# Splitting 512-column matmuls into two of 256 that accumulate in one half of a PSUM bank

## The chip, the cores and the metric

The kernel runs on one core of one Trainium2 chip. The metric is device time of one execution, in microseconds. The core's engines work side by side and wait for each other by semaphores: TensorE (PE in the profile; its weight loads are listed apart as PEld), VectorE (DVE), ScalarE (ACT), GpSimd (POOL) and SyncE (SP), whose queue issues most of the loads from memory.

## The reference

Two layers of a bidirectional encoder on 256 tokens of width 2048, all in float32:

```python
for l in range(DEPTH):
    h = rmsnorm(x, norm_mix[l])
    q, k, v, gate_b, gate_c, u = jnp.split(h @ w_in[l], splits, axis=-1)   # 1024 columns each
    q, k = apply_rope(q), apply_rope(k)                                    # 16 half heads of 64
    o_attn = diff_attention(q, k, v, lam)     # 8 heads: softmax 1 - lam * softmax 2, times v
    o_attn = rmsnorm(o_attn, subln[l]) * (1.0 - lam_init)
    z = gate_c * u
    o_conv = gate_b * (w[0] * z[t - 1] + w[1] * z[t] + w[2] * z[t + 1])    # centred, 3 taps
    x = x + concatenate([o_attn, o_conv]) @ w_out[l]
    h = rmsnorm(x, norm_ffn[l])
    x = x + (silu(h @ w_gate[l]) * (h @ w_up[l])) @ w_down[l]
return rmsnorm(x, norm_final)
```

## The kernel before

**Exactness.** Matmuls run on operands of type fp32r, which keeps fewer bits than float32. Each operand is therefore kept as two parts, a high one (the value rounded to fp32r) and a low one (value minus high part). A product is hi x hi + hi x lo + lo x hi. For weights, ScalarE makes the high part (`whi`) and VectorE the low one (`wlo`). The normed activations stand in `xg`, which holds for each of the 16 slices of the model's width 512 columns: 256 tokens of the high part, then 256 tokens of the low part.

**Blocks and banks.** Work is cut in blocks of 512 output columns. Each layer has 4 blocks for q and k, 2 for v, 6 for the conv path (named gate: two for B, two for C, two for u), 4 for the output projection, and then those of the feed-forward part. A block reads its weights in units of two 128-row slices. PSUM has 8 banks of 512 columns; blocks use banks 0 to 3, the attention and transposes banks 4 to 7.

**Two kinds of product.** The v, output and feed-forward blocks go by tokens (`products_by_tokens`, L2118): activations are the loaded operand, weights stream through in 512 columns, and the result has tokens on partitions. The q/k and gate blocks go by features (`products`, L2092): a 128 x 128 tile of weights is loaded and the tokens stream through, so the result has features on partitions, 4 tiles in 4 banks. There the high weights meet all 512 columns of `xg` at once (L2108): hi x hi lands in the left half of the bank, hi x lo in the right half. The low weights meet only the 256 high columns (L2111), which add to the left half. For every slice TensorE does the two tiles of a pair with high weights, then the same two with low weights; first tiles 0 and 1 for a unit, then 2 and 3.

**Leaving the bank.** The two halves must be added. `low_halves` (L978) on ScalarE copies the right half of each tile's bank to `ev`; `sums` (L1664) on VectorE adds left half and `ev`, into `qk` for a q/k block and into `ev` for a gate block. For B and C, `gate_out` (L1740) then multiplies by the token's RMS factor into `gates`; for u, `conv_products` (L1746) multiplies by the gated C to give z. Each of these steps is counted up on a semaphore: `low_copied`, `bank_free`, `gate_stored`, `z_ready`.

**Order.** The order on each engine is written out by hand; every engine runs its list in order. A block's drain stands in the lists of ScalarE and VectorE behind the splits of the first two units of the next block. TensorE waits in `tile_free` (L2088) before it starts a pair of tiles: the counter `bank_free`, counted up by every last reader of a bank, must have reached the number of tiles up to the one four tiles earlier. In a gate block the attention of one head (mix, scores, two kinds of transposes) is put between units, and VectorE makes sums of feed-forward weights ahead of time (`sums_ahead`, L1380) that ScalarE's queue stores to memory: in some gate blocks one such sum stands between the second and the third tile of the drain. The POOL's queue swaps rows of `qk` for the rotary embedding once a block's drain has been counted (`swap`, L772).

Of the kernel before, what the change touches and what calls it, by code (L numbers as in the profile page):

```python
# [9 lines left out]
ALU = mybir.AluOpType  # L10
# [4 lines left out]
S = 256  # L15
# [146 lines left out]
class Block:  # L162
# [5 lines left out]
    def __init__(self, plan, layer, name, i, by_tokens, units):  # L168
        self.layer, self.name, self.i = layer, name, i
        self.by_tokens, self.units = by_tokens, units  # L170
        self.tiles = QT if by_tokens else BT
        self.tile0, self.low0 = plan.tiles, plan.lows
        plan.tiles += self.tiles
        plan.lows += 0 if by_tokens else BT
        self.load, self.split = {}, {}
        self.first_unit = None
        self.ahead = {}
# [98 lines left out]
class Plan:  # L276
    def __init__(self):
        self.tiles = self.lows = self.units_taken = self.quads = self.pair_count = self.fold_steps = 0

        self.ready_at = []  # L280
        self.by_dve = self.by_pool = 0
# [49 lines left out]
    def split_unit(self, loads, tiles, block=None, last=False, by_pool=False):  # L331
# [22 lines left out]
        else:  # L354
            self.by_dve += 1
            self.ready_at.append(("dve", self.by_dve))
        return n

    def next_place(self):
# [15 lines left out]
def build_program(nc, x, x_t_d, w_in, w_out, w_gu, w_down, consts_d, lambdas_d, tables_d, ident_d, gain_d, out):  # L375
# [146 lines left out]
    first_half_hi = sem("first_half_hi")  # L522
    low_copied = sem("low_copied")
    xg_hi = sem("xg_hi")
# [24 lines left out]
    first_half_ready = sem("first_half_ready")  # L549
    bank_free = sem("bank_free")  # L550
    set_up = sem("set_up")
    warm_set = sem("warm_set")
# [7 lines left out]
    rope_done = sem("rope_done")  # L560
    gate_stored = sem("gate_stored")
    z_ready = sem("z_ready")
    conv_step = sem("conv_step")
# [42 lines left out]
    def wait_for_split(engine, n):  # L606
        kind, count = plan.ready_at[n]
        engine.wait_ge(pool_weights_ready if kind == "pool" else weights_ready, count)

    def batch_number(layer, name, b=0):  # L610
# [17 lines left out]
    with nc.Block() as block:  # L628
# [138 lines left out]
        def _(pool):  # L767
# [4 lines left out]
            def swap(layer, c):  # L772
                blk = at_block[layer, "qk", c]
                pool.wait_ge(bank_free, blk.tile0 + BT)
                if layer * NQK + c > 1:
                    pool.wait_ge(rope_done, layer * NQK + c - 1)
                for r in range(4):
                    pool.dma_start(swaps[c % 2][32 * r:32 * r + 32],
                                   qk[32 * (r ^ 1):32 * (r ^ 1) + 32, c * BT:(c + 1) * BT, :]
                                   ).then_inc(swap_landed[c % 2], 16)  # L780
# [109 lines left out]
        def _(act):  # L890
# [86 lines left out]

            def low_halves(blk, ev_free=None):  # L978
                if ev_free is not None:
                    act.wait_ge(ev_free[0], ev_free[1])  # L980
                for j in range(BT):
                    act.wait_ge(tile_done, blk.tile0 + j + 1)
                    act.activation(ev[:, j, :], bank[blk.bank(j)][:, S:2 * S], ACT.Copy).then_inc(low_copied, 1)

            def squares(norm, c):
                for q in range(QT):
                    if norm == 0:
                        act.wait_ge(x_landed[q], 16)
                    else:
                        act.wait_ge(bank_free, chunk_source(norm, c).tile0 + q + 1)  # L990
                    before = norm * QT * NCH + QT * c + q
# [26 lines left out]
            def conv(layer, u):  # L1018
                for j in range(BT):
                    tap = layer * (3 * CT) + (C_CONV + CT + BT * u + j)  # L1020
                    act.wait_ge(z_ready, layer * CT + (BT * u + j + 1))
                    act.activation(ev[:, j, :], gates[:, CT + BT * u + j, :], ACT.Copy, scale=consts[:, tap:tap + 1]
# [7 lines left out]
            def silu(layer, g, q):  # L1030
# [6 lines left out]
                elif g > 1:  # L1037
                    act.wait_ge(hidden_turned, layer * NGU + g - 1)
                act.wait_ge(bank_free, blk.tile0 + q + 1)
                act.activation(ev[:, QT * (g % 2) + q, :], gate_up_tile(layer, g, q)[:, 0:S], ACT.Silu, scale=rms_tok[:, q:q + 1]  # L1040
# [132 lines left out]

            def gates_stored(layer, n):
                return gate_stored, layer * (2 * CT) + n

            act.dma_start(consts[:], consts_d).then_inc(consts_landed, 16)
# [4 lines left out]
            for layer in range(DEPTH):  # L1182
# [28 lines left out]
                for c in range(1, NQK):  # L1211
                    blk = at_block[layer, "qk", c]
                    split(blk, 0, 2)
                    low_halves(at_block[layer, "qk", c - 1])
                    if layer == 0 and c == 1:
# [11 lines left out]
                split(blk, 0, 2)  # L1227
                low_halves(at_block[layer, "qk", NQK - 1])
                split(blk, 2, UNITS)
# [9 lines left out]
                for b in range(3 * NG):  # L1239
# [5 lines left out]
                    copy_weights(layer, h - 1)  # L1245
                    if b == 1:
                        low_halves(at_block[layer, "gate", 0])
                    elif b > 1:
                        low_halves(at_block[layer, "gate", b - 1], gates_stored(layer, min(b - 1, 2 * NG) * BT))
                    split(blk, 2, 4)  # L1250
# [13 lines left out]
                copy_weights(layer, HEADS - 1)  # L1264
                low_halves(at_block[layer, "gate", 3 * NG - 1], (conv_ready, layer * CT + BT))
                split(blk, 2, 4)
                conv(layer, 1)
                split(blk, 4, 6)
# [95 lines left out]
        def _(dve):  # L1364
# [298 lines left out]

            def sums(blk, qk_block=None, between=None):  # L1664
                for j in range(BT):
                    if j == BT // 2 and between is not None:
                        sums_ahead(between, 1, range(3), 1)
                    dst = ev[:, j, :] if qk_block is None else qk[:, qk_block * BT + j, :]
                    dve.wait_ge(low_copied, blk.low0 + j + 1)
                    dve.tensor_tensor(dst, bank[blk.bank(j)][:, 0:S], ev[:, j, :], ALU.add).then_inc(bank_free, 1)  # L1670

            def rotate(layer, c):
# [66 lines left out]

            def gate_out(layer, g, scale):  # L1740
                blk = at_block[layer, "gate", g]
                for j in range(BT):
                    dve.wait_ge(bank_free, blk.tile0 + j + 1)
                    dve.tensor_tensor(gates[:, g * BT + j, :], ev[:, j, :], scale[:], ALU.mult).then_inc(gate_stored, 1)

            def conv_products(layer, u):  # L1746
                dve.wait_ge(gate_stored, (layer + 1) * 2 * CT)
                for j in range(BT):
                    t = CT + BT * u + j
                    dve.wait_ge(bank_free, at_block[layer, "gate", 2 * NG + u].tile0 + j + 1)  # L1750
                    dve.tensor_tensor(gates[:, t, :], ev[:, j, :], gates[:, t, :], ALU.mult).then_inc(z_ready, 1)

# [107 lines left out]
            for layer in range(DEPTH):  # L1860
# [25 lines left out]
                for c in range(1, NQK):  # L1886
                    blk = at_block[layer, "qk", c]
                    split(blk, 0, 2)
                    if layer == 0 and c == 2:
                        norm_sums(mix)  # L1890
                    sums(at_block[layer, "qk", c - 1], c - 1)
                    sums_ahead(blk, 1, range(3))
# [17 lines left out]
                sums_ahead(blk, 1, range(3))  # L1910
                sums(at_block[layer, "qk", NQK - 1], NQK - 1)
                split(blk, 2, 3)
# [27 lines left out]
                for b in range(1, 2 * NG + 1):  # L1940
                    blk = at_block[layer, "gate", b]
                    split(blk, 0, 2)
                    sums_ahead(blk, 1, range(3))
                    sums(at_block[layer, "gate", b - 1], between=blk)
                    split(blk, 2, 3)
                    gate_out(layer, b - 1, rms_bc if b <= NG else rms2_bc)
                    split(blk, 3, 4)
                    attention_part(layer, blk, b + 2)
                blk = at_block[layer, "gate", 3 * NG - 1]
                split(blk, 0, 2)  # L1950
                sums_ahead(blk, 1, range(3))
                sums(at_block[layer, "gate", 2 * NG])
                split(blk, 2, 3)
                conv_products(layer, 0)
                split(blk, 3, 4)
                conv_neighbours(layer, 0)
# [11 lines left out]
                sums_ahead(blk, 1, range(3))  # L1968
                sums(at_block[layer, "gate", 3 * NG - 1])
                split(blk, 2, 3)  # L1970
                conv_products(layer, 1)
                split(blk, 3, 4)
                conv_neighbours(layer, 1)
# [110 lines left out]
        def _(pe):  # L2084
# [3 lines left out]
            def tile_free(blk, j):  # L2088
                if blk.tile0 + j >= BT:
                    pe.wait_ge(bank_free, blk.tile0 + j + 1 - BT)  # L2090

            def products(blk, ks, moving, halves=range(UNIT_KT)):  # L2092
# [4 lines left out]
                for pair in range(0, BT, 2):  # L2097
# [5 lines left out]
                    for k in ks:  # L2103
                        for i in halves:
                            kt = UNIT_KT * k + i
                            final = k == blk.units - 1 and i == UNIT_KT - 1
                            for j in js:
                                pe.matmul(b[j][:], whi[:, plan.span[blk.split[k]].start + i, w[j]], moving[:, kt, :], start=(kt == 0),  # L2108
                                          stop=False, skip_group_check=True)
                            for j in js:  # L2110
# [138 lines left out]
            def turn_x(norm, c):  # L2249
                pe.wait_ge(bank_free, chunk_source(norm, c).tile0 + QT)  # L2250
                for i in range(BT):
# [38 lines left out]
            def mix(layer, h):  # L2290
                n = layer * HEADS + h
                pe.wait_ge(wt_copied, n + 1)
                if h == 0:

                    pe.wait_ge(bank_free, at_block[layer, "v", 0].tile0 + QT)
                else:
# [287 lines left out]
```

## Time and profile before

| | us |
|---|---|
| median of 3 runs | 2151.37 (2151.27 to 2151.44) |
| the profiled execution | 2151.05 |
| its span, first to last instruction | 2149.3 |

A row of a timeline names the start, the length, the engine, the line and the shapes (output <- inputs, the loaded operand last); xN merges N like instructions that follow each other. The length of a matmul includes the time until its result is out, so matmuls overlap and the distance of two starts tells the pace. In groups by line, busy is the time covered by the group's instructions and the mean is that of one.

### The profile page before, as it was taken

To read this page: it belongs to the slowest core of one execution; us is meant where nothing else is said; L and a number is where in the kernel's file an instruction comes from. 1 tells how busy PE (TensorE), PEld (TensorE's weight loads), DVE (VectorE), ACT (ScalarE), POOL (GpSimd) and SP (SyncE) were. 2 spreads that over 40 slices of the span, in tenths; PEclk is the share of its full clock that TensorE was granted. 3 is DMA by queue.
4 is the path that set the end of the run, shared out by engine and by line. 5 is a ranking of instruction groups with operands and counts; after the bars stand their busy time and mean duration, and the time that the engine had idled before them with its cause. 6 is when DMAs were issued, how large, how long until landed. Compare 5 with 4: busy or idle time off the path is not lost.

```text
span 2149.3 us, 27652 instructions
## 1 busy us (share of the span) xinstructions
PE 2138.9 (100%) x10349; PEld 1783.9 (83%) x10349; DVE 1851.8 (86%) x2149; ACT 1244.7 (58%) x1652; POOL 313.8 (15%) x298
## 2 busy tenths in 40 slices
PE   9999999999999999999999999999999999999998
PEld 7888888788888888888888888888888888888886
DVE  6788887899999988999867788878999998988997
ACT  6445455566666655556554555546666666655564
POOL 0031120211121110000001211202112112000010
PEclk9999999999999999999999999999999999999999
DMA  9768877877786876767757688678678777757685
GB/s 351 241 255 338 335 254 281 270 261 243 268 284 219 279 261 204 228 216 225 239 198 252 253 326 333 247 286 294 222 275 278 248 259 265 254 192 223 218 240 181
DMA packets 171877, 553.25 MB, mean 257 GB/s; under 512 B 19552, under 2 KB 20192, under 8 KB 166752
## 3 DMA queue, kind: packets, MB, share of 16 engines
q1 hardware_dynamic: 149040, 479.33, 62.1%
q0 software_dynamic: 16512, 31.47, 8.3%
q10 hardware_dynamic: 6192, 40.69, 4.7%
q8 instruction: 82, 1.34, 0.2%
q14 instruction: 51, 0.42, 0.0%
HBM read 507.37 MB, written 39.85 MB: 255 GB/s over the span
## 4 chain that ended last, share of the span: by engine, by line
PE 98%; DVE 1%; ACT 0%; issue 0%; ACTq 0%; DVEq 0%
PE bank L2135 15%; PE bank L2136 15%; PE bank L2137 15%; PE bank L2108 14%; PE bank L2148 10%; PE bank L2149 10%; PE bank L2150 10%; PE bank L2111 7%; PE bank L2318 1%; PE bank L2277 1%; PE bank L2300 1%; DVE wlo L1398 1%; PE bank L2256 0%; PE bank L2286 0%; PE bank L2247 0%; PE bank L2307 0%
## 5 line engine op out<-in xcount | busy, mean ns | idle before, releaser
L902 ACT ACTIVATE whi<-raw 128x1024 fp32r<-128x1024 f32 x472 | 484.6, 1056 | 196.2 <-PE bank L2137 109.6
L1390 DVE TENSOR_TENSOR wlo<-raw,whi 128x1024 fp32r<-128x1024 f32 x446 | 538.2, 1231 | 69.0 <-ACT whi L902 68.0
L917 ACT ACTIVATE whi<-raw 128x1024 fp32r<-128x1024 f32 (+1 forms) x368 | 390.4, 1088 | 211.9 <-DVE raw L1413 90.3
L1398 DVE TENSOR_TENSOR wlo<-raw,whi 128x1024 fp32r<-128x1024 f32 (+1 forms) x368 | 452.3, 1260 | 34.6 <-ACT whi L917 31.4
L2108 PE MATMUL bank<-xg,whi 128*128 128x512 f32 x1280 | 407.0, 399 | 0.0
L2135 PE MATMUL bank<-whi,xg 128*128 128x512 f32 x736 | 289.8, 394 | 0.0
L2111 PEld LDWEIGHTS bank<-xg,wlo 128*128 128x128 f32 x1280 | 240.5, 188 | 56.9
L2137 PE MATMUL bank<-whi,xg 128*128 128x512 f32 x736 | 287.0, 390 | 0.0
L2136 PE MATMUL bank<-wlo,xg 128*128 128x512 f32 x736 | 286.8, 390 | 0.0
L2111 PE MATMUL bank<-xg,wlo 128*128 128x256 f32 x1280 | 252.2, 278 | 0.0
L2108 PEld LDWEIGHTS bank<-xg,whi 128*128 128x128 f32 x1280 | 195.1, 189 | 2.4 <-DVE xg L1695 0.7
L2135 PEld LDWEIGHTS bank<-whi,xg 128*128 128x128 f32 x736 | 138.2, 188 | 29.5 <-DVE wlo L1390 1.4
L2135 PE MATMUL bank<-whi,hidden 128*128 128x512 f32 x416 | 162.6, 391 | 0.0
L2137 PEld LDWEIGHTS bank<-whi,xg 128*128 128x128 f32 x736 | 138.2, 188 | 29.0
L2137 PE MATMUL bank<-whi,hidden 128*128 128x512 f32 x416 | 162.0, 389 | 0.0
L2136 PE MATMUL bank<-wlo,hidden 128*128 128x512 f32 x416 | 161.9, 389 | 0.0
L2136 PEld LDWEIGHTS bank<-wlo,xg 128*128 128x128 f32 x736 | 138.3, 188 | 27.6
L2148 PE MATMUL bank<-whi,form_hi_gu 128*128 128x512 f32 x400 | 155.7, 389 | 0.0
L2150 PE MATMUL bank<-whi,form_lo_gu 128*128 128x512 f32 x400 | 155.7, 389 | 0.0
L2149 PE MATMUL bank<-wlo,form_hi_gu 128*128 128x512 f32 x400 | 155.7, 389 | 0.0
L809 POOL DMA_DIRECT2D raw<-w_gu_dram x52 | 45.9, 884 | 561.9 <-DMA raw<-w_gu_dram 507.9
L2148 PE MATMUL bank<-whi,xg 128*128 128x512 f32 x300 | 119.9, 400 | 0.8 <-DVE wlo L1398 0.7
(172 smaller groups left out, 3554.9 us busy)
## 6 DMA issues: line engine op xcount, KB each, us to landing
raw<-w_gu_dram SPq DMA_DIRECT2D x252, 512.0 KB, 6.3
raw<-w_in_dram SPq DMA_DIRECT2D x188, 512.0 KB, 4.7
raw<-w_down_dram SPq DMA_DIRECT2D x140, 512.0 KB, 5.3
sums_kept<-raw ACTq DMA_DIRECT2D x32, 1024.0 KB, 4.0
raw<-w_out_dram SPq DMA_DIRECT2D x64, 512.0 KB, 4.5
raw_gu<-w_gu_dram SPq DMA_DIRECT2D x64, 512.0 KB, 6.4
raw<-w_gu_dram SPq DMA_DIRECT2D x124, 256.0 KB, 5.6
raw<-sums_kept SPq DMA_DIRECT2D x44, 512.0 KB, 5.1
```

The source lines that it names most:

```text
L902: act.activation(whi[:, plan.span[blk.split[k]]], raw_place(slot)[:, half * UNIT_KT:(half + 1) * UNIT_KT, :], ACT.Copy).then_inc(hi_ready, 1)
L917: act.activation(whi[:, plan.span[quad.split[n]]], raw_place(place)[:, tiles, :], ACT.Copy).then_inc(hi_ready, 1)
L1390: dve.tensor_tensor(wlo[:, tiles], raw_place(slot)[:, half * UNIT_KT:(half + 1) * UNIT_KT, :], lo_bits(whi[:, tiles]), ALU.subtract).then_ ...
L1398: dve.tensor_tensor(wlo[:, into], raw_place(place)[:, tiles, :], lo_bits(whi[:, into]), ALU.subtract).then_inc(weights_ready, 1)
L2108: pe.matmul(b[j][:], whi[:, plan.span[blk.split[k]].start + i, w[j]], moving[:, kt, :], start=(kt == 0), stop=False, skip_group_check=True)
L2111: done = pe.matmul(b[j][:, 0:S], wlo[:, plan.span[blk.split[k]].start + i, w[j]], moving[:, kt, 0:S], start=False, stop=final, skip_group_ ...
L2135: pe.matmul(b[:], x_hi, w_hi, start=(n == UNIT_KT * blk.first_unit), stop=False)
L2136: pe.matmul(b[:], x_hi, w_lo, start=False, stop=False)
L2137: done = pe.matmul(b[:], x_lo, w_hi, start=False, stop=final)
L2148: pe.matmul(into[:], x_hi, w_hi, start=start, stop=False)
L2149: pe.matmul(into[:], x_hi, w_lo, start=False, stop=False)
L2150: return pe.matmul(into[:], x_lo, w_hi, start=False, stop=stop)
```

## The change

`products` issues, for each slice and tile, two matmuls of 256 columns with the same high weights, one with the high and one with the low half of `xg`, and both add to the left half of the bank. Each has its own weight load. The right half is not used any more. So `low_halves` and `sums` go: for q and k, ScalarE copies the left half straight to `qk` (`copy_out`); for B and C, VectorE's `gate_out` reads the bank; for u, `conv_products` reads the bank. The split of the third unit moves from ahead of these products to behind them. `low_copied`, `gate_stored` and `z_ready` go; a bank is now freed on one of two counters, `bank_copied` (ScalarE, q/k blocks) or `bank_free` (VectorE, all others), and `wait_for_bank` picks the one and its count for a tile.

```diff
@@ class Block / class Plan
-        self.tile0, self.low0 = plan.tiles, plan.lows
+        self.tile0 = plan.tiles
         plan.tiles += self.tiles
-        plan.lows += 0 if by_tokens else BT
+        for _ in range(self.tiles):
+            plan.free_at.append(plan.next_free("scalar" if name == "qk" else "vector"))
...
+    def next_free(self, engine):
+        self.freed[engine] += 1
+        return engine, self.freed[engine]
...
+    def wait_for_bank(engine, tile):
+
+        by, count = plan.free_at[tile]
+        engine.wait_ge(bank_copied if by == "scalar" else bank_free, count)
...
@@ POOL
             def swap(layer, c):
                 blk = at_block[layer, "qk", c]
-                pool.wait_ge(bank_free, blk.tile0 + BT)
+                wait_for_bank(pool, blk.tile0 + BT - 1)
...
@@ ScalarE
-            def low_halves(blk, ev_free=None):
-                if ev_free is not None:
-                    act.wait_ge(ev_free[0], ev_free[1])
+            def copy_out(blk):
                 for j in range(BT):
                     act.wait_ge(tile_done, blk.tile0 + j + 1)
-                    act.activation(ev[:, j, :], bank[blk.bank(j)][:, S:2 * S], ACT.Copy).then_inc(low_copied, 1)
+                    act.activation(qk[:, blk.i * BT + j, :], bank[blk.bank(j)][:, 0:S], ACT.Copy).then_inc(bank_copied, 1)
...
             def conv(layer, u):
...
-                    act.wait_ge(z_ready, layer * CT + (BT * u + j + 1))
+                    wait_for_bank(act, at_block[layer, "gate", 2 * NG + u].tile0 + j)
...
-                    low_halves(at_block[layer, "qk", c - 1])
+                    copy_out(at_block[layer, "qk", c - 1])
...
-                    if b == 1:
-                        low_halves(at_block[layer, "gate", 0])
-                    elif b > 1:
-                        low_halves(at_block[layer, "gate", b - 1], gates_stored(layer, min(b - 1, 2 * NG) * BT))
...
                 copy_weights(layer, HEADS - 1)
-                low_halves(at_block[layer, "gate", 3 * NG - 1], (conv_ready, layer * CT + BT))
                 split(blk, 2, 4)
+                act.wait_ge(conv_ready, layer * CT + BT)
                 conv(layer, 1)
...
@@ VectorE
-            def sums(blk, qk_block=None, between=None):
...
-            def gate_out(layer, g, scale):
+            def gate_out(layer, g, scale, between):
+
                 blk = at_block[layer, "gate", g]
                 for j in range(BT):
-                    dve.wait_ge(bank_free, blk.tile0 + j + 1)
-                    dve.tensor_tensor(gates[:, g * BT + j, :], ev[:, j, :], scale[:], ALU.mult).then_inc(gate_stored, 1)
+                    if j == BT // 2:
+                        sums_ahead(between, 1, range(3), 1)
+                    dve.wait_ge(tile_done, blk.tile0 + j + 1)
+                    dve.tensor_tensor(gates[:, g * BT + j, :], bank[blk.bank(j)][:, 0:S], scale[:], ALU.mult
+                                      ).then_inc(bank_free, 1)
 
             def conv_products(layer, u):
...
-                    dve.wait_ge(bank_free, at_block[layer, "gate", 2 * NG + u].tile0 + j + 1)
-                    dve.tensor_tensor(gates[:, t, :], ev[:, j, :], gates[:, t, :], ALU.mult).then_inc(z_ready, 1)
+                    dve.wait_ge(tile_done, blk.tile0 + j + 1)
+                    dve.tensor_tensor(gates[:, t, :], bank[blk.bank(j)][:, 0:S], gates[:, t, :], ALU.mult
+                                      ).then_inc(bank_free, 1)
...
-                    sums(at_block[layer, "qk", c - 1], c - 1)
...
                     split(blk, 0, 2)
                     sums_ahead(blk, 1, range(3))
-                    sums(at_block[layer, "gate", b - 1], between=blk)
-                    split(blk, 2, 3)
-                    gate_out(layer, b - 1, rms_bc if b <= NG else rms2_bc)
-                    split(blk, 3, 4)
+                    gate_out(layer, b - 1, rms_bc if b <= NG else rms2_bc, blk)
+                    split(blk, 2, 4)
...
@@ TensorE
             def tile_free(blk, j):
                 if blk.tile0 + j >= BT:
-                    pe.wait_ge(bank_free, blk.tile0 + j + 1 - BT)
+                    wait_for_bank(pe, blk.tile0 + j - BT)
...
                             for j in js:
-                                pe.matmul(b[j][:], whi[:, plan.span[blk.split[k]].start + i, w[j]], moving[:, kt, :], start=(kt == 0),
-                                          stop=False, skip_group_check=True)
+                                for part in (0, S):
+                                    pe.matmul(b[j][:, 0:S], whi[:, plan.span[blk.split[k]].start + i, w[j]],
+                                              moving[:, kt, part:part + S], start=(kt == 0 and part == 0), stop=False,
+                                              skip_group_check=True)
                             for j in js:
                                 done = pe.matmul(b[j][:, 0:S], wlo[:, plan.span[blk.split[k]].start + i, w[j]], moving[:, kt, 0:S],
                                                  start=False, stop=final, skip_group_check=True)
```

## Rows read from the trace of the kernel before

**Rows 1.** The page, part 1: busy us (share) and instructions, by engine.

```profile
PE 2138.9 (100%) x10349; PEld 1783.9 (83%) x10349; DVE 1851.8 (86%) x2149; ACT 1244.7 (58%) x1652; POOL 313.8 (15%) x298
```

**Rows 2.** The page, part 4: the chain that ended last, by engine.

```profile
PE 98%; DVE 1%; ACT 0%; issue 0%; ACTq 0%; DVEq 0%
```

**Rows 3.** The chain of waits by line, whole span.

```profile
by line: PE bank L2135 14.8%; PE bank L2136 14.7%; PE bank L2137 14.7%; PE bank L2108 14.0%; PE bank L2148 10.1%; PE bank L2149 9.9%; PE bank L2150 9.9%; PE bank L2111 6.9%; PE bank L2318 0.9%; PE bank L2277 0.7%; PE bank L2300 0.7%; DVE wl
```

**Rows 4.** Instructions by line: shapes, count | busy us, mean ns | idle.

```profile
L2108 PE MATMUL bank<-xg,whi 128*128 128x512 f32 x1280 | 407.0, 399 | 0.0
L2111 PE MATMUL bank<-xg,wlo 128*128 128x256 f32 x1280 | 252.2, 278 | 0.0
L2111 PEld LDWEIGHTS bank<-xg,wlo 128*128 128x128 f32 x1280 | 240.5, 188 | 56.9
L2300 PEld LDWEIGHTS bank<-v_tok,wt 128*128 128x128 f32 x128 | 15.8, 191 | 0.3
```

**Rows 5.** Stages: length, busy PE, PEld, DVE, ACT, POOL, clock, DMA.

```profile
1098.93:1121.22 22.29, 22.29 (x131) 19.45 (x129) 14.39 (x15) 9.47 (x12) 2.03 (x4) 1.00 0.67 228
169.32:194.32 25.00, 25.00 (x156) 21.88 (x155) 21.37 (x34) 13.04 (x27) 4.50 (x6) 1.00 0.89 336
```

**Rows 6.** Timeline of TensorE (start us, length us), one step of that q/k block.

```profile
1098.93 0.63 PE L2108 MATMUL bank<-xg,whi 128*128 128x512 f32 x2
1099.39 0.40 PE L2111 MATMUL bank<-xg,wlo 128*128 128x256 f32 x2
1099.62 0.40 PE L2108 MATMUL bank<-xg,whi 128*128 128x512 f32 x1
```

**Rows 7.** Timeline of TensorE's weight loads, the mix of a head and what follows.

```profile
174.78 0.97 PEld L2300 LDWEIGHTS bank<-v_tok,wt 128*128 128x128 f32 x8
175.67 0.30 PEld L2108 LDWEIGHTS bank<-xg,whi 128*128 128x128 f32 x2
```

**Rows 8.** Timeline of TensorE, products by tokens, a start and the twelfth after it.

```profile
101.26 0.39 PE L2135 MATMUL bank<-whi,xg 128*128 128x512 f32 x1
...
103.98 0.39 PE L2135 MATMUL bank<-whi,xg 128*128 128x512 f32 x1
```

**Rows 9.** Timeline of TensorE, scores of a head, second pair and last pair.

```profile
153.91 0.28 PE L2277 MATMUL bank<-k_lo,q_hi 64*128 64x256 f32 x2
...
154.38 0.28 PE L2277 MATMUL bank<-k_hi,q_lo 64*128 64x256 f32 x2
```

**Rows 10.** Instructions grouped by line, the drains of the banks.

```profile
L983 ACT ACTIVATE ev<-bank 128x256 f32<-128x256 f32 x80 | 26.4, 382 | 97.1 <-PE bank L2111 97.1
L1670 DVE TENSOR_TENSOR ev<-bank,ev 128x256 f32<-128x256 f32 x48 | 18.0, 418 | 11.5 <-ACT ev L983 11.3
L1670 DVE TENSOR_TENSOR qk<-bank,ev 128x256 f32<-128x256 f32 x32 | 12.1, 419 | 30.1 <-ACT ev L983 30.1
L1744 DVE TENSOR_TENSOR gates<-ev,rms_bc 128x256 f32<-128x256 f32 x32 | 11.4, 417 | 0.0
L1751 DVE TENSOR_TENSOR gates<-ev,gates 128x256 f32<-128x256 f32 x16 | 5.7, 418 | 0.0
```

**Rows 11.** Timelines of VectorE and TensorE where one gate block follows another.

```profile
1261.41 0.76 DVE L1670 TENSOR_TENSOR ev<-bank,ev 128x256 f32<-128x256 f32 x2 [0.77 <-ACT ev L983]
1264.66 0.75 DVE L1670 TENSOR_TENSOR ev<-bank,ev 128x256 f32<-128x256 f32 x2
1263.63 0.62 PE L2108 MATMUL bank<-xg,whi 128*128 128x512 f32 x2
1266.42 0.40 PE L2108 MATMUL bank<-xg,whi 128*128 128x512 f32 x1
```

**Rows 12.** Timelines of VectorE and TensorE at the output projection's start, layer 0.

```profile
293.92 1.26 DVE L1670 TENSOR_TENSOR ev<-bank,ev 128x256 f32<-128x256 f32 x3
294.03 0.39 PE L2111 MATMUL bank<-xg,wlo 128*128 128x256 f32 x2
294.48 0.47 PE L2135 MATMUL bank<-whi,mixed 128*128 128x512 f32 x1
```

More of the change, by code:

```diff
@@ L277, in __init__ @@
     def __init__(self):
-        self.tiles = self.lows = self.units_taken = self.quads = self.pair_count = self.fold_steps = 0
+        self.tiles = self.units_taken = self.quads = self.pair_count = self.fold_steps = 0
+        self.free_at, self.freed = [], {"scalar": 0, "vector": 0}
         self.ready_at = []
@@ L522, in build_program @@
     first_half_hi = sem("first_half_hi")
-    low_copied = sem("low_copied")
     xg_hi = sem("xg_hi")
@@ L550, in build_program @@
     bank_free = sem("bank_free")
+    bank_copied = sem("bank_copied")
     set_up = sem("set_up")
@@ L560, in build_program @@
     rope_done = sem("rope_done")
-    gate_stored = sem("gate_stored")
-    z_ready = sem("z_ready")
     conv_step = sem("conv_step")
@@ L989, in squares @@
                     else:
-                        act.wait_ge(bank_free, chunk_source(norm, c).tile0 + q + 1)
+                        wait_for_bank(act, chunk_source(norm, c).tile0 + q)
                     before = norm * QT * NCH + QT * c + q
@@ L1038, in silu @@
                     act.wait_ge(hidden_turned, layer * NGU + g - 1)
-                act.wait_ge(bank_free, blk.tile0 + q + 1)
+                wait_for_bank(act, blk.tile0 + q)
                 act.activation(ev[:, QT * (g % 2) + q, :], gate_up_tile(layer, g, q)[:, 0:S], ACT.Silu, scale=rms_tok[:, q:q + 1]
@@ L1172, in head_out @@
                                ).then_inc(o_hi, 1)
-            def gates_stored(layer, n):
-                return gate_stored, layer * (2 * CT) + n
             act.dma_start(consts[:], consts_d).then_inc(consts_landed, 16)
@@ L1227, in _ @@
                 split(blk, 0, 2)
-                low_halves(at_block[layer, "qk", NQK - 1])
+                copy_out(at_block[layer, "qk", NQK - 1])
                 split(blk, 2, UNITS)
@@ L1662, in fold @@
                 dve.tensor_tensor(resid[:, :, right], resid[:, :, right], two, ALU.add).then_inc(fold_step, 1)
-            def sums(blk, qk_block=None, between=None):
[L1665 to L1670, printed above, removed]
             def rotate(layer, c):
@@ L1738, in v_out @@
                                       ALU.mult).then_inc(bank_free, 1)
-            def gate_out(layer, g, scale):
+            def gate_out(layer, g, scale, between):
                 blk = at_block[layer, "gate", g]
                 for j in range(BT):
-                    dve.wait_ge(bank_free, blk.tile0 + j + 1)
-                    dve.tensor_tensor(gates[:, g * BT + j, :], ev[:, j, :], scale[:], ALU.mult).then_inc(gate_stored, 1)
+                    if j == BT // 2:
[3 more added lines that the diff above has]
+                                      ).then_inc(bank_free, 1)
             def conv_products(layer, u):
-                dve.wait_ge(gate_stored, (layer + 1) * 2 * CT)
+                blk = at_block[layer, "gate", 2 * NG + u]
+                wait_for_bank(dve, at_block[layer, "gate", 2 * NG - 1].tile0 + BT - 1)
                 for j in range(BT):
                     t = CT + BT * u + j
-                    dve.wait_ge(bank_free, at_block[layer, "gate", 2 * NG + u].tile0 + j + 1)
-                    dve.tensor_tensor(gates[:, t, :], ev[:, j, :], gates[:, t, :], ALU.mult).then_inc(z_ready, 1)
+                    dve.wait_ge(tile_done, blk.tile0 + j + 1)
+                    dve.tensor_tensor(gates[:, t, :], bank[blk.bank(j)][:, 0:S], gates[:, t, :], ALU.mult
+                                      ).then_inc(bank_free, 1)
             def conv_neighbours(layer, u):
@@ L1910, in _ @@
                 sums_ahead(blk, 1, range(3))
-                sums(at_block[layer, "qk", NQK - 1], NQK - 1)
                 split(blk, 2, 3)
@@ L1951, in _ @@
                 sums_ahead(blk, 1, range(3))
-                sums(at_block[layer, "gate", 2 * NG])
-                split(blk, 2, 3)
                 conv_products(layer, 0)
-                split(blk, 3, 4)
+                split(blk, 2, 4)
                 conv_neighbours(layer, 0)
@@ L1968, in _ @@
                 sums_ahead(blk, 1, range(3))
-                sums(at_block[layer, "gate", 3 * NG - 1])
-                split(blk, 2, 3)
                 conv_products(layer, 1)
-                split(blk, 3, 4)
+                split(blk, 2, 4)
                 conv_neighbours(layer, 1)
@@ L2249, in turn_x @@
             def turn_x(norm, c):
-                pe.wait_ge(bank_free, chunk_source(norm, c).tile0 + QT)
+                wait_for_bank(pe, chunk_source(norm, c).tile0 + QT - 1)
                 for i in range(BT):
@@ L2293, in mix @@
                 if h == 0:
-                    pe.wait_ge(bank_free, at_block[layer, "v", 0].tile0 + QT)
+                    wait_for_bank(pe, at_block[layer, "v", 0].tile0 + QT - 1)
                 else:
```

## The prediction

> **What bounds the kernel now.** I read the page first: TensorE is busy for the whole span, VectorE for 86%, ScalarE for 58% [rows 1]. A share of busy time doesn't say who waits for whom, so the chain of waits comes next: 98% of the time that leads to the last instruction is TensorE's own [rows 2], and by line the two matmul lines which the change edits, L2108 and L2111, hold 14.0% and 6.9%, some 449 us [rows 3]. In the table by stage, the second q/k block of layer 1 takes 22.29 us with TensorE busy throughout, VectorE for 14.39 and ScalarE for 9.47 us, at the full clock level of 2.4 GHz (1.00 in the PEclk column). VectorE has 35% and ScalarE 58% of that block free, and in the second gate block of layer 0, where VectorE is busiest (21.37 of 25.00 us), TensorE is busy throughout as well [rows 5]. So what they lose is worth nothing while TensorE never waits for them, and the whole question is the time of TensorE's own instruction stream.
>
> **What one step of that stream takes.** A step is two output tiles at one 128-row slice of the contraction: two 512-column matmuls (L2108), then two 256-column ones (L2111). A block holds 16 slices x 2 tile pairs = 32 steps, so a step takes 22.29 / 32 = 696.6 ns; the kernel has 1280 / 2 = 640 steps [rows 4] (10 blocks in each of 2 layers), 446 us. Inside a step, from the starts in the timeline, the two long matmuls take 0.46 us and the two short ones 0.23 us [rows 6].
>
> **The change, part by part.**
>
> *The matmuls.* A step goes from 4 matmuls (512, 512, 256, 256 columns) to 6 of 256. The columns stay 1536, which is 640 ns at 2.4 GHz, and each matmul has its own weight load: loads and matmuls are equal in number now, 10349 of each [rows 1], though the products by tokens use the same weights twice in a row. So 1280 matmuls and 1280 loads are added. Are the loads hidden? The recorded load lasts 188 ns [rows 4], more than there is from one short matmul to the next. But in the mix, where a load is recorded at 191 ns [rows 4], 8 of them in a row start 0.89 us / 8 = 111 ns apart [rows 7], so a load doesn't hold the engine for its recorded time; 111 ns is under the 115 ns between short matmuls [rows 6]. They stay hidden, by only a few nanoseconds. If that cover went, 4 new or shortened matmuls a step would each wait for up to 188 - 111 = 77 ns more, 4 x 77 x 640 = 197 us; the short ones of today, which need a load each as well, show nothing like it.
>
> What does a 256-column matmul take in a long row of its kind? No row shows exactly that, so I bound it by four readings. (a) Half of a 512-column matmul in the products by tokens, whose starts are 2.72 / 12 = 226.7 ns apart: 113.3 [rows 8]. (b) The short ones as they stand, which come in twos behind two long ones: 0.23 / 2 = 115 by the starts, 6.9% of 2149.3 us / 1280 = 115.9 by the chain; I take 115.4 [rows 3, 6]. (c) The scores, the only run of 256-column fp32r matmuls one after another: two row groups at once, five starts 0.47 / 4 = 117.5 apart [rows 9]. (d) A fixed cost for every matmul: (696.6 - 640) / 4 = 14.2 ns, so 106.7 + 14.2 = 120.8. By (d) the 226.7 of the 512-column ones (213.3 + 13.4) fits almost exactly. Break-even is 696.6 / 6 = 116.1.
>
> I take (c), 117.5: it is the one row in which the pace must sustain itself. In (b) two short ones may run ahead and be paid back by the next long one; what makes me suspect it is that the long ones take 0.46 / 2 = 230 or more [rows 6], against 226.7 in the products by tokens [rows 8]. A step becomes 6 x 117.5 = 705.0 ns, +8.4, times 640: **+5.4 us**. The ends are 113.3 (-16.8 ns a step, -10.7 us) and 120.8 (+28.2, +18.1 us).
>
> *Draining the bank.* ScalarE loses 48 copies of a gate tile's low half at 0.382 us; the 32 copies for q and k stay, now as the whole drain and straight into qk. VectorE loses 80 additions at 0.418 (48 + 32); its 48 gate and conv products stay at 0.418 and read the bank in place of ev [rows 10]. Reading a bank costs no more: the additions that go read one, in the same 0.418. All of it lies beside TensorE, so I cost it at nothing. The cover is the time between a drain's end and the matmul that reuses the bank. At a gate boundary the additions for the first two tiles end at 1261.41 + 0.76 = 1262.17 and TensorE returns at 1263.63; those for the other two end at 1265.41 and TensorE starts them at 1266.42 [rows 11]. That is 1.46 and 1.01 us to spare. After the change each drain drops one hop (q and k end at ScalarE's copy; the gate product starts without waiting for one), so the spare time grows. In the gate blocks one prepared sum (three VectorE instructions) still stands between the second and third tile, as before; that it becomes the bound would take a delay of a full microsecond.
>
> *Two waits that can shrink.* At the start of the output projection TensorE waits for the first drain of the last gate block: the last pair of short matmuls starts at 294.03, the next line at 294.48, not 294.26, and the addition that frees the bank started at 293.92 [rows 12]. That is 0.22 us in each layer, 0.44 us at most to be had and, if conv_products gets there later by one such instruction, 0.84 to be lost. VectorE has four additions fewer to do in the block before; I take -0.2 us.
>
> *Waits.* No new one is added to TensorE: the wait on a freed bank moves to a counter of the engine that frees it. ScalarE's wait for conv_ready moves from ahead of low copies that are gone to the second conv, behind two splits; VectorE counts it up at the end of the block before; queued behind it on ScalarE are the convolution's middle taps and the splits from the fifth unit on. The POOL's row swaps for rope start on ScalarE's copy, about one addition (0.42 us) earlier. SP's loads and their order are untouched. What is late next is TensorE itself.
>
> **Sum.** +5.4 - 0.2 = +5.2 us. The profiled execution took 2151.05 us (span 2149.3, 1.75 around it) and becomes 2156.3; the median of the runs is 2151.37, 0.32 above, so I predict **2156.6 us**.
>
> **Rivals.**
>
> *Each matmul has a fixed cost (d).* 6 x 120.8 = 724.8, +18.1 us: 2169.3 with the waits. For it: one constant explains both the 226.7 [rows 8] and the 696.6 [rows 5] within 1 ns a matmul. Against it: short ones start 115 apart today, and the scores 117.5.
> The Trainium skill, TensorE: Matmul & The Clock Gate, section Back-to-back issue gap, gives the gap as the columns at 2.4 GHz plus about 2.5 ns for each matmul, whatever its length, which also speaks against splitting; by it the 1280 extra matmuls would add 3.2 us, an estimate, and the time would be 2154.4. The products by tokens show 13.4 ns over the columns, not 2.5 [rows 8], so its size doesn't hold here, while its form is the rival's.
>
> *Not slower: the pairs of today already show the sustained pace (b).* A load can start only when the matmul before it has started, so no debt is carried from one to the next and 115.4 holds through the block: 6 x 115.4 = 692.4, -4.2 ns a step, -2.7 us, and 2148.5. It decides as soon as the pace stays under 116.1. For it: it is the pace of these very blocks. Against it: the long ones' excess of some 4 to 6 ns each over those in the products by tokens [rows 6, 8].
>
> *Columns alone count (a).* The long ones' excess vanishes too: 680 a step, -10.7 us, 2140.5. Against it: nothing in these blocks runs at that pace today.
>
> *The lighter VectorE shows.* It can give only time in which TensorE waits. The chain has 2% outside TensorE [rows 2], and both blocks looked at have none [rows 5]; what I found is the 0.44 us [rows 12]. Not a case of its own.
>
> **Chances and range.** Pace near 117.5: 0.40 (2153.5 to 2159.5, from 116.8 to 118.4). Fixed cost: 0.27. Pace of the pairs: 0.24. Columns alone: 0.06. The rest, either way: 0.03. About 0.2% (4.3 us) is what a measurement tells from no change, so slower begins at 2155.7: just over half of the likeliest case, all of the fixed cost and a little of the rest make 0.50. The lower part of the likeliest case and three quarters of the pairs make 0.35, the rest 0.15. The range from 2145 to 2171 takes in the fixed cost and the pairs and leaves out columns alone.
>
> **What would show it.** In the profile after: the same q/k block [rows 5] longer than 22.29 us (22.56 for 117.5, 23.2 for a fixed cost, 22.16 for the pairs), with TensorE still busy throughout. Six starts in a step at an even distance. L2108's successor with 2560 matmuls of 256 columns and as many loads. VectorE's busy time down by about 80 x 0.418 = 33 us and ScalarE's by 18 us, with no gain from either. I am wrong if TensorE shows waits on the freed bank inside the gate blocks, if the loads stand alone on the chain, or if a block takes less than 22.2 us.

## The result and the profile after

The changed kernel takes 2165.1 us (2165.02 to 2165.14, 3 runs) against 2151.37: ratio 1.0064, 95% interval 1.0041 to 1.0087. It is slower by 13.7 us, as forecast in sign and within the range, but by more than twice the 5.2 us that I gave; the time lies next to the rival of a fixed cost (2169.3).

The page of the changed kernel, parts 1 and 4, which answer to [rows 1, 2]:

```profile
PE 2152.1 (99%) x11629; PEld 1854.7 (86%) x11629; DVE 1822.6 (84%) x2069; ACT 1231.6 (57%) x1604; POOL 302.5 (14%) x298
...
PE 97%; DVE 2%; ACT 0%; issue 0%; DMA 0%; ACTq 0%; DVEq 0%
```

There are 1280 matmuls and 1280 loads more. VectorE is busy for 29 us less and ScalarE for 13 us less, and neither buys anything: 97% of the chain is TensorE's, 98% before. By line [rows 3]:

```profile
by line: PE bank L2127 14.5%; PE bank L2129 14.5%; PE bank L2128 14.4%; PE bank L2099 14.3%; PE bank L2140 9.8%; PE bank L2142 9.6%; PE bank L2141 9.6%; PE bank L2103 7.1%; DVE wlo L1398 1.0%; PE bank L2310 0.9%; PE bank L2269 0.7%; PE bank
```

L2099 is the successor of L2108, L2103 of L2111. Together they hold 21.4% of 2163.2 us, 463 us, where they held 449. In groups by line, with the drains (L990 copies q and k, L1739 makes the gates), for [rows 4, 10]:

```profile
L2099 PE MATMUL bank<-xg,whi 128*128 128x256 f32 x2560 | 416.1, 285 | 0.5 <-DVE wlo L1693 0.5
L2099 PEld LDWEIGHTS bank<-xg,whi 128*128 128x128 f32 x2560 | 352.5, 192 | 2.6 <-DVE xg L1687 0.9
L2103 PE MATMUL bank<-xg,wlo 128*128 128x256 f32 x1280 | 257.7, 283 | 0.0
L2103 PEld LDWEIGHTS bank<-xg,wlo 128*128 128x128 f32 x1280 | 199.5, 192 | 0.0
...
L1739 DVE TENSOR_TENSOR gates<-bank,rms_bc 128x256 f32<-128x256 f32 x32 | 12.0, 417 | 4.5 <-PE bank L2103 4.5
L990 ACT ACTIVATE qk<-bank 128x256 f32<-128x256 f32 x32 | 10.5, 381 | 48.8 <-PE bank L2103 48.8
```

The idle column shows the direction: the drains wait for TensorE, and TensorE's products wait 0.5 us in all, at the kernel's start. The two stages of [rows 5], with the same columns:

```profile
1106.52:1129.56 23.04, 23.04 (x194) 23.04 (x193) 12.94 (x11) 9.47 (x12) 2.03 (x4) 1.00 0.64 219
173.07:198.74 25.67, 25.67 (x221) 25.40 (x220) 20.11 (x30) 12.07 (x23) 4.51 (x6) 1.00 0.93 347
```

The q/k block takes 0.75 us longer, the gate block 0.67, both with TensorE busy throughout. If every block grew as the one of its kind that is shown, eight q/k blocks and twelve gate blocks make 8 x 0.75 + 12 x 0.67 = 14.0 us; 0.44 us of waits are gone, which leaves 13.6 of the 13.9 us by which the span grew. The timeline of TensorE, at the start of the output projection [rows 12] and in a q/k block [rows 6]:

```profile
301.16 0.40 PE L2103 MATMUL bank<-xg,wlo 128*128 128x256 f32 x2
301.40 0.40 PE L2127 MATMUL bank<-whi,mixed 128*128 128x512 f32 x1
...
1109.16 0.40 PE L2103 MATMUL bank<-xg,wlo 128*128 128x256 f32 x2
1109.40 0.64 PE L2099 MATMUL bank<-xg,whi 128*128 128x256 f32 x4
1109.88 0.40 PE L2103 MATMUL bank<-xg,wlo 128*128 128x256 f32 x2
```

Two starts are 0.24 us from the next kind, four 0.48: 120 ns each, and 32 x 6 x 120.0 = 23.04 us is the whole block. The old short matmuls were 115 apart. At 301 us the line after the last pair follows at once; the wait of 0.22 us is gone.

### The profile page after: what moved, and what is told of

It is laid out like the page before. It is cut to its first block, busy times and chain, and to the rows that moved or that the text cites. A ratio compares the mean times of both kernels' runs of the same rounds, so it can differ in the third digit from the quotient of the medians.

```text
span 2163.2 us, 30076 instructions
## 1 busy us (share of the span) xinstructions
PE 2152.1 (99%) x11629; PEld 1854.7 (86%) x11629; DVE 1822.6 (84%) x2069; ACT 1231.6 (57%) x1604; POOL 302.5 (14%) x298
## 4 chain that ended last, share of the span: by engine, by line
PE 97%; DVE 2%; ACT 0%; issue 0%; DMA 0%; ACTq 0%; DVEq 0%
PE bank L2127 15%; PE bank L2129 14%; PE bank L2128 14%; PE bank L2099 14%; PE bank L2140 10%; PE bank L2142 10%; PE bank L2141 10%; PE bank L2103 7%; DVE wlo L1398 1%; PE bank L2310 1%; PE bank L2269 1%; PE bank L2292 1%; PE bank L2248 0%; PE bank L2278 0%; ACT whi L926 0%
## 5 line engine op out<-in xcount | busy, mean ns | idle before, releaser
L2099 PE MATMUL bank<-xg,whi 128*128 128x256 f32 x2560 | 416.1, 285 | 0.5 <-DVE wlo L1693 0.5
L2099 PEld LDWEIGHTS bank<-xg,whi 128*128 128x128 f32 x2560 | 352.5, 192 | 2.6 <-DVE xg L1687 0.9
L2103 PE MATMUL bank<-xg,wlo 128*128 128x256 f32 x1280 | 257.7, 283 | 0.0
L2103 PEld LDWEIGHTS bank<-xg,wlo 128*128 128x128 f32 x1280 | 199.5, 192 | 0.0
```

What stands on the lines that cost most here:

```text
L2099: pe.matmul(b[j][:, 0:S], whi[:, plan.span[blk.split[k]].start + i, w[j]], moving[:, kt, part:part + S], start=(kt == 0 and part == 0), st ...
L2103: done = pe.matmul(b[j][:, 0:S], wlo[:, plan.span[blk.split[k]].start + i, w[j]], moving[:, kt, 0:S], start=False, stop=final, skip_group_ ...
```

## The experiments

Three theories, made after the result, stand against each other. Theory A, the rival of a fixed cost with its size taken from [rows 8]: an fp32r matmul costs its columns at 2.4 GHz and a fixed 13.3 ns. Theory B: columns cost 17/16 of their time, and a row of loads sustains one in 120 ns. Theory C: the drain has a part in it. Each kernel ran beside the kernel before on the same chip.

**The matmuls split alone.** On the kernel before; each half of the bank is opened with a start flag of its own, which changes the sums in q, k and the gates, not the stream of instructions:

```diff
-                                pe.matmul(b[j][:], whi[...], moving[:, kt, :], start=(kt == 0), ...)
+                                for part in (0, S):
+                                    pe.matmul(b[j][:, part:part + S], whi[...], moving[:, kt, part:part + S], start=(kt == 0), ...)
```

> The kernel before with only the matmuls split: each 512-column one becomes two of 256, which write the two halves of the bank as before, so the drain with its second addition stays. Theory A, a fixed cost for every matmul (a 256-column one takes 106.7 + 13.3 = 120.0 ns in a long row, a 512-column one 213.3 + 13.3 = 226.7): the whole rise comes from here, the q/k block of 22.29 us takes 23.04, and the time is 2165.5 us, the changed kernel's 2165.1 and the 0.4 us of two waits at the output projection that stay. Theory B, a row of loads with nothing long between them sustains one in 120 ns, while columns cost 17/16 of their time: the same 23.04 us and 2165.5. Theory C, part of the rise comes from the new drain (a bank freed later, a wait on two counters): below 2164, by that part.

Measured: 2165.51 us, ratio 1.0064 (1.0052 to 1.0077). The stage of a q/k block:

```profile
1107.15:1130.19 23.04, 23.04 (x195) 23.04 (x193) 14.46 (x15) 9.48 (x12) 2.03 (x4) 1.00 0.63 215
```

The whole rise is here, with the old drain and VectorE at 14.46 us, against 14.39 before [rows 5]. C falls.

**The drain alone.** On the changed kernel:

```diff
-                                for part in (0, S):
-                                    pe.matmul(b[j][:, 0:S], whi[...], moving[:, kt, part:part + S], ...)
+                                pe.matmul(b[j][:], whi[...], moving[:, kt, :], start=(kt == 0), ...)
```

> The changed kernel with the matmuls of the kernel before: 512 columns into the whole bank, while the drain reads the left half alone, so high weights times low activations is left out of q, k and the gates. Theories A and B: the drain is worth only the waits at the output projection, 2150.9 us, 0.4 under before, and q/k blocks stay at 22.29 us. Theory C: above 2152.5.

Measured: 2151.45 us, ratio 0.9999 (0.9990 to 1.0008): no change that the runs can tell. Two stages, and the start of the output projection in the timeline:

```profile
1098.56:1120.85 22.29, 22.29 (x130) 19.45 (x129) 12.88 (x11) 9.48 (x12) 2.03 (x4) 1.00 0.67 228
169.25:194.25 25.00, 25.00 (x157) 21.88 (x155) 20.09 (x30) 11.97 (x23) 4.51 (x6) 1.00 0.90 339
```

```profile
293.96 0.39 PE L2101 MATMUL bank<-xg,wlo 128*128 128x256 f32 x2
294.19 0.40 PE L2125 MATMUL bank<-whi,mixed 128*128 128x512 f32 x1
```

Both blocks keep their length to 0.01 us. 294.19 - 293.96 = 0.23, where it was 0.45 [rows 12]: the trace shows the 0.22 us that the total is too coarse to show.

**320 columns, and 384.** On the changed kernel, N = 320 or 384:

```diff
-                                for part in (0, S):
-                                    pe.matmul(b[j][:, 0:S], whi[...], moving[:, kt, part:part + S], ...)
+                                pe.matmul(b[j][:, 0:N], whi[...], moving[:, kt, 0:N], start=(kt == 0), ...)
...
-                                done = pe.matmul(b[j][:, 0:S], wlo[...], moving[:, kt, 0:S], ...)
+                                done = pe.matmul(b[j][:, 0:N], wlo[...], moving[:, kt, 0:N], ...)
```

> The changed kernel with four matmuls of 320 columns in a step (high weights and low weights each meet the first 320 columns of the activations) in place of six of 256: part of high times low is left out, and a part of low times low is added that the drain doesn't read. A length between 256 and 512 tells a fixed cost from a share of the columns. Theory A: 133.3 + 13.3 = 146.7 ns each, a step 586.7, a q/k block 18.77 us, in all 2151 - 640 x 110 ns = 2081 us. Theory B: 133.3 x 17/16 = 141.7 ns each (over the 120 of a load), a step 566.7, a block 18.13 us, 2068 us.

> As with 320 columns, with 384: four matmuls a step that see the first 384 columns of the activations; part of high times low is left out. Theory A: 160 + 13.3 = 173.3 ns each, a q/k block without waits 32 x 693.3 ns = 22.19 us. A share of the columns (17/16): 170.0 ns, 21.76 us. The columns are as many as before (1536), and so are the matmuls of a step, so by theory A such blocks can't be shorter than 22.19 us in any mix of lengths.

Measured with 320: 2102.22 us, ratio 0.977 (0.9752 to 0.9788), neither 2081 nor 2068. The stages say why; first a block without waits, then two others:

```profile
1072.92:1091.70 18.78, 18.78 (x131) 18.78 (x129) 12.76 (x11) 9.48 (x12) 2.03 (x4) 1.00 0.83 287
27.63:49.16 21.53, 19.33 (x131) 18.79 (x129) 9.77 (x10) 14.38 (x28) 2.22 (x4) 1.00 0.95 354
198.99:222.20 23.21, 22.55 (x161) 21.72 (x160) 20.70 (x31) 12.00 (x24) 4.51 (x6) 1.00 0.98 370
```

18.78 / 128 = 146.7 ns: A's figure to the last digit, not B's 141.7. In the others TensorE is no longer busy throughout, the DMA share is 0.95 and 0.98, and loads of weights (`raw<-w_in_dram`) stand on the chain of waits:

```profile
by line: PE bank L2125 15.2%; PE bank L2127 15.1%; PE bank L2126 15.0%; PE bank L2138 10.3%; PE bank L2140 10.1%; PE bank L2139 10.1%; PE bank L2098 3.1%; PE bank L2101 3.1%; DMA raw<-w_in_dram 3.0%; DVE wlo L1390 1.9%; DMA sums_kept<-raw 1
```

This much faster, TensorE outruns its weights, and most of the 21 us that are missing from A's sum are waits. The waits of TensorE (for which line, in all, times, longest) name the drain too:

```profile
PE bank L2098 <- DVE gates L1739: 7.0, 12, 1.0
PE bank L2098 <- DVE wlo L1390: 4.4, 5, 1.2
PE bank L2125 <- DVE gates L1748: 2.1, 2, 1.1
```

Of 18.1 us of such waits in all (1.9 in the kernel before), 9.5 are for VectorE's gate products and 7.4 for its splits of weights. In the gate block shown VectorE is busy for 20.70 of 23.21 us, so here, unlike in the kernel before, a lighter VectorE might be worth something. How much of the loss is the loads' and how much VectorE's, no run tells apart.

With 384, 2149.88 us in one run. The q/k block:

```profile
1098.25:1120.44 22.19, 22.19 (x130) 22.19 (x130) 12.85 (x11) 9.47 (x12) 2.03 (x4) 1.00 0.68 231
```

22.19 / 128 = 173.4 ns, where A has 173.3. With the 226.7 of 512 columns [rows 8] and the 120.0 of 256, four lengths lie on columns / 2.4 GHz + 13.3 ns, with a granted clock of 1.00 in the stages shown. B falls.

**Long and short in turn.** On the kernel before:

```diff
                             for j in js:
                                 pe.matmul(b[j][:], whi[...], moving[:, kt, :], ...)
-                            for j in js:
                                 done = pe.matmul(b[j][:, 0:S], wlo[...], moving[:, kt, 0:S], ...)
```

> The kernel before with the order inside a step changed from long, long, short, short to long, short, long, short; nothing is left out. Theory A: the four costs add up whatever their order, 693 to 697 ns a step, 2149.3 to 2151.6 us, although the starts may shift between long and short. Theory B: every load of a short one now lies behind a long one, so no load is late and only columns count: 2 x (226.7 + 113.3) = 680 ns a step, a q/k block of 21.8 us, 2140.7 us.

Measured: 2153.4 us, ratio 1.0008 (0.9999 to 1.0016). Two stages and a stretch of the timeline:

```profile
1100.91:1123.10 22.19, 22.19 (x131) 19.57 (x129) 14.49 (x15) 9.63 (x13) 2.03 (x4) 1.00 0.68 230
170.45:195.51 25.06, 25.06 (x156) 21.88 (x155) 21.40 (x34) 13.11 (x28) 4.52 (x6) 1.00 0.89 335
```

```profile
1109.92 0.39 PE L2108 MATMUL bank<-xg,whi 128*128 128x512 f32 x1
1110.15 0.28 PE L2110 MATMUL bank<-xg,wlo 128*128 128x256 f32 x1
1110.27 0.39 PE L2108 MATMUL bank<-xg,whi 128*128 128x512 f32 x1
```

The q/k block is 226.7 + 120.0 = 346.7 ns times 64, to the digit; B's 21.8 us is not there. The total lies above A's range, though. The gate block shown grew by 0.06 us, and the first two q/k blocks of layer 0 take 22.88 and 22.61 us, where the kernel before has 22.37 and 22.29. What the order changes there was not followed up.

**Long ones first, then four short ones.** On the kernel before:

```diff
                         for i in halves:
                             kt = UNIT_KT * k + i
-                            final = k == blk.units - 1 and i == UNIT_KT - 1
                             for j in js:
                                 pe.matmul(b[j][:], whi[...], moving[:, kt, :], ...)
+                        for i in halves:
+                            kt = UNIT_KT * k + i
+                            final = k == blk.units - 1 and i == UNIT_KT - 1
                             for j in js:
                                 done = pe.matmul(b[j][:, 0:S], wlo[...], moving[:, kt, 0:S], ...)
```

> The kernel before with the order changed inside a unit of two slices: its four long matmuls first, then its four short ones; nothing is left out. Theory A (every matmul costs its columns and 13.3 ns; a short one can start early behind a long one, and the next long one pays it back): the sum stays, 693 to 697 ns a step, a q/k block without waits 22.19 to 22.29 us, and in the row of four the later short ones come 120 ns apart, not 115. Theory D, which I took for the likeliest not-slower case (the pairs of the kernel before show the true cost of a short one): all four come 115 ns apart.

Measured: 2153.07 us, ratio 1.0007 (0.9997 to 1.0017). The timeline:

```profile
1110.39 1.09 PE L2107 MATMUL bank<-xg,whi 128*128 128x512 f32 x4
1111.32 0.64 PE L2113 MATMUL bank<-xg,wlo 128*128 128x256 f32 x4
1111.80 1.09 PE L2107 MATMUL bank<-xg,whi 128*128 128x512 f32 x4
```

Four short ones take 0.48 us, 120 each, not 115: the pairs of the kernel before did not show the true cost, and D, my not-slower rival, falls. But the four long ones take 0.93 us, 232.5 ns each, so A's sum fails here. The block:

```profile
1100.57:1123.03 22.46, 22.46 (x131) 19.63 (x129) 14.44 (x15) 9.47 (x12) 2.03 (x4) 1.00 0.66 226
```

That is 702 ns a step, where A allowed 693 to 697. A mix of lengths costs 0 to 9 ns a step over A's 693.3, by its order: 693.3 in turn, 696.6 as the kernel before has it, 702 grouped; equal lengths cost nothing over it. Why the order matters stays open.

**bf16.** On the changed kernel, all matmuls of a step read bf16, first as every second half-word with 256 and 320 columns, then side by side from one constant tile:

```diff
-                                    pe.matmul(b[j][:, 0:S], whi[..., w[j]], moving[:, kt, part:part + S], ...)
+                                    pe.matmul(b[j][:, 0:S], half(whi)[..., half_cols(P * j, P)], half(moving)[:, kt, half_cols(part, S)], ...)
```

> The changed kernel with the six matmuls of a step on bf16: each operand is read as the upper half-word of its four bytes (every second half-word), so the lower bits of all products by features are left out. If the 13.3 ns belong to fp32r: the pace falls to what the loads allow, 109 to 111 ns in the transposes and the mix of the kernel before, a step of at most 666 ns and a q/k block without waits of 21.3 us or less. If any matmul pays them: 120 ns and 23.04 us as in the changed kernel. If reading every second half-word is slow, above 120 ns, and nothing follows.

> Four matmuls of 320 columns in a step, as in the fp32r kernel of that length, on the upper half-words read as bf16; the lower bits and part of high times low are left out. With 256 columns bf16 took 113.3 ns, 6.7 over its columns. A fixed cost of the type: 133.3 + 6.7 = 140.0 ns, a q/k block without waits 32 x 560 = 17.92 us. A share of the columns (17/16): 141.7 ns, 18.13 us. A floor set by the loads at 113: 133.3 to 136 ns.

> The changed kernel with the six matmuls of a step on bf16 operands that lie side by side (one constant tile for weights and activations, from the first gate block on), so the products by features are left out there; the first q and k of layer 0 stay fp32r. If the 6.7 ns over the columns come from reading every second half-word: less than 113.3 ns, down to the 109 of the transposes. If they are bf16's own or a floor: 113.3 ns and a q/k block of 21.76 us in layer 1, as before.

Measured, one run each: 2139.65, 2094.4 and 2130.93 us. A q/k block of layer 1 with 256 columns, the same with 320, and the timeline with the operands side by side:

```profile
1092.87:1114.63 21.76, 21.76 (x194) 18.42 (x192) 12.85 (x11) 9.45 (x12) 2.04 (x4) 1.00 0.70 239
```

```profile
1069.69:1087.61 17.92, 17.92 (x130) 12.29 (x128) 12.76 (x11) 9.47 (x12) 2.03 (x4) 1.00 0.83 287
```

```profile
1099.91 0.60 PE L2102 MATMUL bank<-ident 128*128 128x256 bf16 x4
1100.35 0.38 PE L2107 MATMUL bank<-ident 128*128 128x256 bf16 x2
...
1101.87 0.38 PE L2102 MATMUL bank<-ident 128*128 128x256 bf16 x2
```

A q/k block of layer 1 with the operands side by side, and a row of transposes in the kernel before:

```profile
1116.00:1136.96 20.96, 20.96 (x195) 18.79 (x193) 12.85 (x12) 9.45 (x12) 1.94 (x4) 1.00 0.66 226
```

```profile
345.66 1.03 PE L2256 MATMUL bank<-ident,resid 128*128 128x128 f32 x8
```

21.76 / 192 = 113.3 ns and 17.92 / 128 = 140.0: in both 6.7 ns over the columns, again a constant. None of the three outcomes expected of 256 columns came: the block is neither at 21.3 us or less, nor at 23.04, nor above. Side by side, 18 starts take 1.96 us and a block 20.96 / 192 = 109.2 ns each, 2.5 over the columns. That is at most 2.5 ns of fixed cost and not shown to be one: there is only one length, and the eight transposes, with half the columns, come 109 ns apart as well ((1.03 - 0.27) / 7, the last one's own length being 0.27), so whatever paces them, the loads perhaps, could pace these too. The fixed cost is neither that of any matmul nor of the count of loads alone: with the same six loads a step it is 13.3 ns in fp32r, 6.7 in bf16 at every second half-word, and at most 2.5 in bf16 side by side. Which of the two reads it belongs to, that of the weights or that of the tokens, stays open; both changed together, and side by side they also came from one constant tile.

None of the runs points to a version that would beat both kernels by what can be measured. The lighter drain is worth 0.44 us and needs the whole sum in the left half, which here takes the split; and 1536 columns in four fp32r matmuls are at 22.19 us a q/k block, at best 0.1 us under the kernel before.

## Why the prediction was right in sign and low in size

- *What bounds the kernel*: right. Only TensorE's stream counted; 29 us less of VectorE changed the total by nothing that can be told.
- *Loads stay hidden*: right. The profile lists them busy for all 23.04 us of a block, yet 256 columns lie on the same line as 320, 384 and 512, where the loads have time to spare; a bound by loads would lift the shortest off it.
- *The pace of a 256-column matmul, term (c), 117.5 ns*: this is the step that was mis-sized. It measured 120.0, so a step grew by 23.4 ns and not 8.4, 15.0 us by 640 steps and not 5.4. The scores were the wrong row: they run in two row groups of 64 rows at once, unlike the blocks; what makes them 2.5 ns faster no run shows. The right sign was luck in part: 117.5 lay only 1.4 ns over the break-even of 116.1, and the margin came from a row that these blocks don't follow. The products by tokens were the right one [rows 8], as their 13.4 ns over the columns is the constant that held at every length.
- *Reading (d)* had the mechanism and was 0.8 ns a matmul too high: it spread all of the 56.6 ns over the four matmuls [rows 5], and 3.3 of those belong to the mix of lengths, not to the constant.
- *Reading (b)*, the pairs at 115 ns: the suspicion against it was right. With a longer row of short ones they come 120 apart. Starts tell the pace only over a whole period of the pattern.
- *Busy times* of the drain's engines fell by 29 and 13 us, not 33 and 18. I multiplied the length of one instruction by their count, but the profile counts time in which two overlap once: 80 copies of 0.382 us cover 26.4 us, not 30.6 [rows 10]. Nothing in the sum hung on it.
- *The bounds of the likeliest case*: by my own paces of 116.8 and 118.4 they are 2153.9 and 2160.0, about half a microsecond over those given.
- *The waits*: up to 0.44 us was to be had and 0.2 was taken; all of it came.
- *Gate blocks* grew by 0.67, not 0.75 us. The 0.08 us lie around the pieces of attention; I did not find out why.
- *The page's rule*, the Trainium skill, TensorE: Matmul & The Clock Gate, section Back-to-back issue gap: columns plus about 2.5 ns, which the section gives for a matmul by itself and not for pairs of a load and a matmul as here. Its form, columns and a constant, held wherever the lengths were equal, in fp32r and in bf16 at every second half-word. Its 2.5 is not the 13.3 of fp32r; the 109.2 ns of bf16 side by side would fit it, but don't show it, as the transposes have that pace too.

The waits that I named as proof of being wrong did not appear: no matmul of the gate blocks waits on a freed bank in the changed kernel. These are all the waits of its TensorE that the profile lists:

```profile
PE bank L2140 <- DVE wlo L1398: 1.2, 2, 0.7
PE bank L2239 <- DVE unused_squares L1854: 1.2, 1, 1.2
PE bank L2099 <- DVE wlo L1693: 0.5, 1, 0.5
```

## What to carry to other kernels

Work out what a matmul costs over its columns from the steadiest row of equal ones with the same operand type and layout, and take that constant for each matmul that a change adds. Splitting matmuls to relieve another engine pays only if TensorE waits for that engine, and for longer than the added matmuls cost. In a pattern of different lengths, divide the whole period; the distance of two starts inside it can be off by several per cent in either direction.

## What was not expected of the hardware

The fixed part depends on how the operands are read: 13.3 ns in fp32r at 256, 320, 384 and 512 columns, 6.7 ns in bf16 at every second half-word at 256 and 320, at most 2.5 ns in bf16 side by side, seen at 256 alone. And equal lengths run at the constant's pace exactly (120.0, 146.7, 173.3), while three orders of the same long and short ones gave 693, 697 and 702 ns a step.
